# A fused two-block kernel: the last two chunks of two output projections, taken token tile by token tile

## The reference, cut to what matters

```python
def diff_mixer(h, w_in, lam, subln_g, w_out, cos, sin, lambda_init):
    proj = jnp.einsum('btd,de->bte', h, w_in)
    ...
    o = sweep_query_blocks(block, T)
    o = rms_norm(o, subln_g) * (1.0 - lambda_init)
    return jnp.einsum('bte,ed->btd', o.reshape(bsz, T, ODD_MIX), w_out)

def moba_attention(h, w_qkv, w_o, rel_bias):
    ...
    return o @ w_o

# behind the first:  h = h + diff_mixer(...); h = h + sq_relu_mlp(rms_norm(h, g), w_up, w_down)
# behind the second: x = x + g1 * y; h = modulate(rmsnorm(x, norm_mlp), sh2, sc2); x = x + g2 * mlp(h)
```

## Time and profile before

| what | value |
| --- | --- |
| median of 3 runs | 1152.67 us (1152.41 to 1152.84) |
| the profiled execution | 1151.84 us, its span 1150.0 us |
| TensorE busy | 1116.5 us of the span (97%) |
| VectorE, ScalarE busy | 838.3 us, 587.5 us |

### The profile page before, as it was taken

One profiled execution on the slowest core, in us unless ns is written; L12 is line 12 of the kernel. 1 busy time (PEld: TensorE's weight loads), 2 busy tenths in 40 slices (PEclk: granted clock), 3 DMA queues, 4 the chain that ended last, 5 costly groups with the idle time before them and its releaser, 6 DMA issues.

```text
span 1150.0 us, 16198 instructions
## 1 busy us (share of the span) xinstructions
PE 1116.5 (97%) x6407; PEld 937.6 (82%) x6407; DVE 838.3 (73%) x1378; ACT 587.5 (51%) x909; POOL 56.8 (5%) x105
## 2 busy tenths in 40 slices
PE   5999999999999999999999899999999999999997
PEld 5857568888888887888888798888879878888886
DVE  5679358888786776798788889877884557666654
ACT  6444465444445676744444574444466655544442
POOL 1101000000000000010000001000011000000000
PEclk9999999999999999999999999999999998999999
DMA  8526268977844335698876359878636442755530
GB/s 306 197 98 229 66 240 320 354 282 274 309 160 146 121 137 183 244 399 310 294 286 237 136 186 387 304 281 302 238 124 219 146 157 97 274 195 202 184 110 37
DMA packets 39291, 252.20 MB, mean 219 GB/s; under 512 B 6712, under 2 KB 6912, under 8 KB 10544
## 3 DMA queue, kind: packets, MB, share of 16 engines
q1 hardware_dynamic: 26640, 189.67, 45.8%
q0 software_dynamic: 12576, 61.51, 14.8%
HBM read 249.37 MB, written 4.25 MB: 221 GB/s over the span
## 4 chain that ended last, share of the span: by engine, by line
PE 87%; DVE 8%; ACT 2%; issue 1%; DMA 1%; SPq 0%; DVEq 0%; ACTq 0%
PE bank L1331 51%; PE bank L1479 25%; PE bank L1767 2%; PE bank L1531 2%; PE bank L1556 1%; PE bank L1594 1%; PE bank L1411 1%; DVE x L855 1%; PE bank L1750 1%; ACT vo L550 1%; DVE us L882 1%; DVE work L853 1%; DVE wlo L835 1%; PE bank L1833 1%; PE bank L1668 1%
## 5 line engine op out<-in xcount | busy, mean ns | idle before, releaser
L835 DVE TENSOR_TENSOR wlo<-raw,whi 128x2048 fp32r<-128x2048 f32 (+2 forms) x143 | 324.4, 2273 | 59.6 <-ACT whi L540 59.5
L540 ACT ACTIVATE whi<-raw 128x2048 fp32r<-128x2048 f32 (+2 forms) x143 | 270.5, 1896 | 2.3 <-DMA raw<-in_stream 1.4
L1331 PE MATMUL bank<-whi,hh 128*128 128x512 f32 x544 | 214.0, 393 | 0.0
L1331 PE MATMUL bank<-wlo,hh 128*128 128x512 f32 x544 | 212.4, 390 | 0.0
L1331 PE MATMUL bank<-whi,hl 128*128 128x512 f32 x544 | 211.8, 389 | 0.0
L1479 PE MATMUL bank<-us,whi 128*128 128x512 f32 x832 | 197.0, 389 | 0.0
L1479 PEld LDWEIGHTS bank<-us,whi 128*128 128x128 f32 x832 | 156.2, 188 | 32.4
L1331 PE MATMUL bank<-us,whi 128*128 128x256 f32 x880 | 166.9, 290 | 0.0
L1331 PEld LDWEIGHTS bank<-us,whi 128*128 128x128 f32 x880 | 136.9, 191 | 8.1 <-issue 7.4
L1331 PE MATMUL bank<-whi,us 128*128 128x256 f32 (+2 forms) x512 | 131.7, 341 | 12.0 <-DVE wlo L835 6.3
L1331 PE MATMUL bank<-us,wlo 128*128 128x256 f32 x440 | 124.3, 282 | 0.0
(11 more groups left out here) (208 smaller groups left out, 1132.7 us busy)
## 6 DMA issues: line engine op xcount, KB each, us to landing
raw<-in_stream SPq DMA_DIRECT2D x176, 1024.0 KB, 5.0
qk<-in_w_mod POOLq DMA_DIRECT2D x48, 1024.0 KB, 5.7
bias_rows<-bias_heads POOLq DMA_DIRECT2D x4, 768.0 KB, 17.7
u<-bias_rows POOLq DMA_DIRECT2D x16, 128.0 KB, 2.8
vo<-feature_rows POOLq DMA_DIRECT2D x3, 512.0 KB, 9.1
raw<-in_stream SPq DMA_DIRECT2D x2, 696.0 KB, 10.5
x<-in_x SPq DMA_DIRECT2D x2, 512.0 KB, 4.7
cb<-feature_rows POOLq DMA_DIRECT2D x2, 512.0 KB, 6.3
```

The costliest lines, as they stand in the source:

```text
L540: nc.scalar.activation(whi[:, c % RING, 0:w], raw[:, n % RING, 0:w], ACT.Copy).then_inc(hi_ready, 1)
L835: nc.vector.tensor_tensor(wlo[:, c % RING, 0:w], raw[:, raw_index(c) % RING, 0:w], whi[:, c % RING, 0:w].bitcast(fp32), ALU.subtract).then ...
L1331: ins = mm(out, st, mv, start=start and i == 0, stop=stop and i == 2, skip_group_check=True)
```

## The change

For both mixers (`CLOSED` names them) `project_beside` now takes only c0 and c1 whole. Then come c2 for t0, with its quarters (14, 0) and (14, 1); what the table has for quarters (14, 2) and (14, 3); the wait for c3's weights and operand; c3 for t0; c2 for t1; the turning of t0; c3 for t1. Nothing is computed differently, and ScalarE's and VectorE's lists stay as they are.

```diff
+CLOSED = ('d', 'b')
...
-                for c in range(3):
+                for c in range(2 if ph in CLOSED else 3):
                     pe.wait_ge(lo_ready, m0 + c + 1)
                     pe.wait_ge(ol_ready, 4 * r + c + 1)
                     add_rows(m0 + c, e, *parts(c), c == 0, False, steps=lambda q: steps(c, q))
+                if ph in CLOSED:
+
+                    pe.wait_ge(lo_ready, m0 + 3)
+                    pe.wait_ge(ol_ready, 4 * r + 3)
+                    add_rows(m0 + 2, e, *parts(2), False, False, (0,), steps=lambda q: steps(2, q))
+                    for q in (2, 3):
+                        steps(2, q)
+                    pe.wait_ge(lo_ready, m0 + 4)
+                    pe.wait_ge(ol_ready, 4 * r + 4)
+                    add_rows(m0 + 3, e, *parts(3), False, True, (0,))
+                    add_rows(m0 + 2, e, *parts(2), False, False, (1,))
+                    norm(e, 0)
+                    add_rows(m0 + 3, e, *parts(3), False, True, (1,))
+                    return
                 pe.wait_ge(lo_ready, m0 + 4)
                 pe.wait_ge(ol_ready, 4 * r + 4)
                 add_rows(m0 + 3, e, *parts(3), False, True)
```

## The result

The changed kernel takes 1157.0 us (median of 20 runs, 1154.43 to 1161.22), the kernel before 1153.03 us beside it (20 runs, 1151.25 to 1158.87). The ratio is 1.0036, with a 95% interval from 1.0025 to 1.0048: 4.1 us slower, between 2.9 and 5.5. That is inside the range on record (1152.4 to 1157.2), 0.2 us from its end, and outside the forecast's own range (1154.2 to 1156.2).

What follows compares the result with a forecast made beforehand. TensorE, busy 97% of the span, was taken as the bound. Differential mixer +2.8 (1.3 + 1.5 clock) and block attention -0.2 gave +2.6 us on the median 1152.67: 1155.3 us, range 1152.4 to 1157.2.

Steps and rivals of the forecast that it cites:

- the forecast's own range: Whole kernel: 1154.2 to 1156.2 us, one short low-clock stretch in each mixer, give or take one; chance 0.45.
- The later chunk release: Differential mixer: transfers on POOL's queue go out some 3.8 us later; costed at nothing, 3.8 us at most.
- Holes of 1.3 and 2.5 us: Differential mixer: TensorE idles 1.3 us before `pair_out` and 2.5 us before c3, which starts at 454.68 as before.
- The price without the clock, +1.3: Differential mixer at full clock: 2.77 us of matmuls not done, 0.86 and 0.35 won back, +1.3 us.
- 0.4, then 3.45 us: Block attention: a new TensorE wait of 0.4 us before c3, and the hole before t0's turning growing from 1.77 to 3.45.
- -0.75: Block attention: the gain of only 0.75 us had the clock before stayed up.
- Rival 3: VectorE takes the residual and `pair_lower` ahead of splitting halves: sum -2.3 us, 1150.4 us; chance 0.05.
- The clock falls behind both holes: Both mixers: holes with only transposes (4.3 and 4.45 us) bring the granted clock to 0.50 behind them.
- the 1.5 us for one short low stretch: Behind each mixer's hole: matmuls at half speed cost 1.5 us, from a 1.4 to 2.85 us span.
- rival 2: Long low-clock stretches (5.7 us) in one or both mixers: up to +5.3 us, 1156.5 to 1158.0 us; chance 0.22.
- -0.2: Block attention with a short low stretch: t1's turning at 966.7 + 1.5 = 968.2 against 968.43, so -0.2 us.
- +2.6: Whole kernel: +2.8 us in the differential mixer and -0.2 in the block attention, 0.22% slower.

Runs made afterwards that it cites:

- e1: The kernel before with the new order in the differential mixer alone; 1156.77 us, ratio 1.0026.
- e3: e1 plus 15 matmuls nobody reads in the differential mixer's two holes, 5 ahead of `pair_out` and 10 ahead of c3; 1154.89 us, ratio 1.0007.
- e7: The changed kernel with unread matmuls in the holes of both mixers and around the turning behind the pooling mixer; 1153.83 us, ratio 1.0001 to the kernel before.
- e4: e2 plus 14 matmuls nobody reads ahead of the turning of t0 in the block attention; 1151.45 us, ratio 0.9979.
- e8: e2 with VectorE's last two splitting halves moved behind t0's bias, plus unread matmuls there and behind the pooling mixer; 1152.28 us, ratio 0.9989.
- e11: e8's order and moved splitting halves, without any unread matmuls; 1150.44 us, ratio 0.9975 to the kernel before.
- e9: The changed kernel plus unread matmuls between the pooling mixer's small matmuls and around the turning behind it; 1158.10 us, ratio 1.0037 to the kernel before.
- e2: The kernel before with the new order in the block attention alone; 1154.09 us, ratio 1.0003.
- e12: e11 plus, in the differential mixer's old order, VectorE's `pair_lower` ahead of its last two splitting halves; 1151.98 us, ratio 0.9986 to the kernel before.

## Why the prediction was right, and where it was off

- **What bounds, and the two places.** Right. The stretches outside D, P and B are the same to 0.1 us; stage P's 4.0 us are taken up under the sum. The later chunk release, costed at nothing, cost nothing: P in e1 is 199.69 us against 199.89.
- **Holes of 1.3 and 2.5 us in the differential mixer, c3 no earlier.** Right: 1.05 and 2.36 us. The price without the clock, +1.3, was +1.2 (e3) and +1.1 (e7).
- **Block attention, 0.4, then 3.45 us; residual held by the splitting.** Right in kind: 0.16 and 3.22 us. -0.75 against an execution whose clock holds was -0.9 (e4). Rival 3, that VectorE would be free at once, did not come about with this change, and the gain it promised there was got by moving the splitting (e8, e11).
- **The clock falls behind both holes.** Right, and shown by e3, e4 and e7. The term that was mis-sized is the 1.5 us for one short low stretch in the differential mixer: it cost 1.6 us in e1 (3.4 us long) and 2.5 in the changed kernel (6.8 us long). I had given the long stretch to rival 2 because c3's matmuls would not come late; but they started 1.3 us into it, and it was long. In e1 and e9 it began 0.5 us behind c3's first matmul (454.30 and 454.82 in e1) and was short; how often each comes is not shown. In the block attention -0.2 was reckoned from 21.51, an execution with a long low stretch; against 20.93, with a short one or none, the new order gives -0.1 (e2) or +0.3 (e9). Of four executions of the old order there with its holes empty, two had the long one.
- **The sum.** +2.6 was forecast; D and B add up to +2.95 in the profile, and the runs say 4.1 (2.9 to 5.5). Without the runs of the lowest granted clock the medians are 1155.7 and 1152.7, +3.0, as much as D and B. The other 1 us, by this estimate, goes with those runs: 8 of 20 with the change, 25 of 113 before. The one of them that was profiled has its low stretch in the pooling mixer, for which the prediction had no term; P varies by 4 us between executions, also in kernels without the loss in D (204.09 and 204.07 in e11 and e12). Whether the change makes such runs more frequent is not settled; e9 was to show it and did not.
- **Where the median fell.** 1157.0 is not in the forecast's own range but in that of rival 2 (1156.5 to 1158.0, chance 0.22). Its case, a long low stretch in one of the places, is what the profile shows in D, at 2.5 us where it had 2.85; e1 and e9 show the forecast's short one. That the median came out inside the whole range, by 0.2 us, owes something to luck, since 1 us of it has no term in the sum.
- **The Trainium skill**, "TensorE: Matmul & The Clock Gate", spoke against the change: a gap between bursts brings the lower clock (Part 1, HAM oscillation), and transposes don't count as busy in the same way (Part 4). e1 and e3 agree: four transposes in a hole of 3.4 us did not keep the clock, fifteen matmuls around them did.

## What to carry to other kernels

Work that is moved to cover a later wait uncovers an earlier one: count the idle time on both sides, and ask which engine sets the end of the wait. Here the chain had two ends on VectorE. In the block attention the new order on TensorE alone gave 0.1 us at most (0.9 with fill that kept the clock up), and with two halves of VectorE's own work moved into a wait for a root it gave 2.3 us in the stage, or 1.1 behind a low stretch (e12). In the differential mixer VectorE's reordering alone gave 0.6 us. New holes on TensorE cost what isn't won back behind them (1.2 us here), and the low stretch behind them costs again about half of what it covers of matmuls (1.6 and 2.5 us), unless a later wait hides that. Matmuls that nobody reads show in one run how much of a loss is the clock's; they are a probe, and where they stood among working matmuls they cost time themselves (1.4 us in e9).

## What was not expected of the hardware

- Low stretches of up to 10.2 us in the pooling mixer, where TensorE was not idle ahead of them: they begin among small matmuls, of which 32 took 6.31 us instead of 3.75 in the changed kernel's profile. Why the clock falls there in some executions and not in others is not shown.
- A low stretch of 3.4 us behind the block attention's hole cost nothing (B 20.93 with and without it), since TensorE waited for VectorE at the next turning anyway.
- The runs of one kernel spread over 5 to 10 us (1151.25 to 1158.87 before), and within a kernel the slow ones are those of the lower mean granted clock. A stretch at half clock in the pooling mixer is large enough to explain it (4 us in P), but in none of the experiments was the spread removed on purpose.
